# The last column block of three phases of a two-block transformer layer, run one half of the tokens after the other

## The reference, cut to what matters

```python
# first_block, after attention and the gated recurrence (projections gate_a, gate_b)
merged = (sigmoid(gate_a) * (y_attn @ w_attn_branch) + sigmoid(gate_b) * (y_hgrn @ w_hgrn_branch))
x = x + rms_norm(merged @ w_out, g_mix_post)
h = rms_norm(x, g_ffn_pre)
gate, up = split(h @ w_gate_up)
x = x + rms_norm((silu(gate) * up) @ w_down, g_ffn_post)
ple_gate = sigmoid(rms_norm(x, g_ple_pre) @ w_ple_gate)
e = (p @ w_ple_proj) * ple_gate
x = x + rms_norm(e, g_ple_post)

# second_block, twice (l = 0, 1); mod comes from c and w_ada
shift, scale, gate = split(silu(c) @ w_ada[l] + b_ada[l])
h = layernorm(x) * (1 + scale) + shift
u_f, z_f, cq, ckv, k_r, z_a = split(h @ w_in[l])
y = concat([fourier_mix(u_f) * silu(z_f), latent_attention(cq, ckv, k_r) * silu(z_a)]) @ w_out[l]
x = layernorm(ALPHA * x + gate * y) * ln_g[l] + ln_b[l]
```

## Time and profile before

| what | us |
|---|---|
| median of 3 runs | 2385.27 (2381.05 to 2387.98) |
| the profiled execution: device time | 2383.35 |
| its span (first to last instruction) | 2381.5 |
| TensorE busy | 2235.6 (94%) |
| VectorE busy | 1530.5 (64%) |
| ScalarE busy | 1102.9 (46%) |
| GpSimd busy | 103.0 (4%) |

### The profile page before, as it was taken

The page is one execution under the profiler, slowest core; times in us unless marked ns, Lnnn a source line. Parts: engine busy times, 40 slices in busy tenths (PEclk is TensorE's granted clock), DMA queues, the critical chain, the costliest instruction groups (busy, mean ns, idle before and its releaser), DMA issues.

```text
span 2381.5 us, 26442 instructions
## 1 busy us (share of the span) xinstructions
PE 2235.6 (94%) x10514; PEld 1860.3 (78%) x10514; DVE 1530.5 (64%) x1820; ACT 1102.9 (46%) x1497; POOL 103.0 (4%) x97
## 2 busy tenths in 40 slices
PE   8999999999897999999999999796999995999996
PEld 6788888887786788878887888675888774888875
DVE  5665476748776776677777777676365556545555
ACT  5566455433344444444433444555465343545542
POOL 1000000001100000000000001011000002000001
PEclk9999999999999999999999999898999997999998
DMA  6544654477885888888888887673464463544463
GB/s 220 182 133 133 194 168 145 135 242 263 271 275 204 287 279 283 280 288 294 287 283 281 299 282 262 201 248 117 136 189 123 156 232 97 161 151 141 149 230 106
DMA packets 233659, 500.60 MB, mean 210 GB/s; under 512 B 15696, under 2 KB 25600, under 8 KB 232128
## 3 DMA queue, kind: packets, MB, share of 16 engines
q1 hardware_dynamic: 229520, 485.64, 62.4%
q0 software_dynamic: 2416, 11.85, 1.4%
q10 hardware_dynamic: 1600, 1.43, 0.2%
HBM read 496.74 MB, written 2.12 MB: 209 GB/s over the span
## 4 chain that ended last, share of the span: by engine, by line
PE 52%; DMA 18%; issue 11%; DVE 11%; ACT 6%; POOL 1%; SPq 0%; POOLq 0%; ACTq 0%; DVEq 0%
PE bank L210 50%; DMA raw<-in_w_gate_up 7%; DVE wl L231 5%; DMA raw<-in_w_down 4%; ACT wh L227 4%; DVE arena L239 3%; DMA raw<-in_w_out 3%; PE bank L218 2%; DVE arena L231 2%; ACT arena L227 1%; DMA raw<-in_w_ple_gate 1%; DMA raw<-in_w_hgrn_branch 1%; POOL arena L231 1%; DMA raw<-in_w_attn_branch 1%; DMA raw<-in_w_ada 1%
## 5 line engine op out<-in xcount | busy, mean ns | idle before, releaser
L231 DVE TENSOR_TENSOR wl<-raw,wh 128x1024 fp32r<-128x1024 f32 (+1 forms) x732 | 892.2, 1226 | 613.3 <-ACT wh L227 606.5
L227 ACT ACTIVATE wh<-raw 128x1024 fp32r<-128x1024 f32 (+1 forms) x732 | 763.0, 1048 | 957.9 <-PE bank L210 365.3
L210 PE MATMUL bank<-wh,hh 128*128 128x512 f32 (+1 forms) x1616 | 640.9, 397 | 24.4 <-DVE wl L231 8.2
L210 PE MATMUL bank<-wh,hl 128*128 128x512 f32 (+1 forms) x1616 | 629.9, 390 | 0.0
L210 PE MATMUL bank<-wl,hh 128*128 128x512 f32 (+1 forms) x1616 | 629.4, 389 | 0.0
L210 PE MATMUL bank<-wh,ah 128*128 128x512 f32 (+1 forms) x1312 | 515.0, 393 | 17.5 <-DVE wl L231 16.2
L210 PE MATMUL bank<-wl,ah 128*128 128x512 f32 (+1 forms) x1312 | 509.9, 389 | 0.0
L210 PE MATMUL bank<-wh,al 128*128 128x512 f32 (+1 forms) x1312 | 509.8, 389 | 0.0
L210 PEld LDWEIGHTS bank<-wh,hh 128*128 128x128 f32 x1616 | 307.0, 190 | 90.2 <-DVE wl L231 11.6
L210 PEld LDWEIGHTS bank<-wh,hl 128*128 128x128 f32 x1616 | 306.5, 190 | 63.2
L210 PEld LDWEIGHTS bank<-wl,hh 128*128 128x128 f32 x1616 | 307.1, 190 | 59.1
(11 more groups left out here) (100 smaller groups left out, 685.9 us busy)
## 6 DMA issues: line engine op xcount, KB each, us to landing
raw<-in_w_in SPq DMA_DIRECT2D x264, 512.0 KB, 3.8
raw<-in_w_ada SPq DMA_DIRECT2D x192, 512.0 KB, 4.8
raw<-in_w_gate_up SPq DMA_DIRECT2D x176, 512.0 KB, 4.9
raw<-in_w_out SPq DMA_DIRECT2D x96, 512.0 KB, 4.9
raw<-in_w_down SPq DMA_DIRECT2D x88, 512.0 KB, 5.1
raw<-in_w_ple_gate SPq DMA_DIRECT2D x32, 512.0 KB, 5.4
raw<-in_w_attn_branch SPq DMA_DIRECT2D x16, 512.0 KB, 5.0
raw<-in_w_hgrn_branch SPq DMA_DIRECT2D x16, 512.0 KB, 5.2
```

Source lines behind the costliest of these rows:

```text
L210: return put("pe", lambda e: e.matmul(o, l, r, start=start, stop=stop_, skip_group_check=skip), w, sig, size(r) / 2400.0 * (4 if r.dtype = ...
L227: return e.activation(o, i, f, scale=scale, **k)
L231: return put(eng, lambda e: e.tensor_tensor(o, a, b, op), w, cost=vcost(eng, o))
```

## The change

Three blocks now run *by halves*: the last `wo` block (`split="half"`: units 0 to 3 for both halves of the tokens, then units 4 to 7 for m = 0 and again for m = 1), the last `pgate` block and the last `wo2` block of each layer (`split="last"`: all 8 units for m = 0, then all 8 for m = 1). What follows such a block is emitted per half (`ev_post_half`, `ev_pg_last`, `ev_o_last`). So that 8 units of weights can stay, blocks 1 to 3 of these phases borrow the idle operand H as four more slots (`lend`, `release`); the slots are one queue now, and `take_item` is called by their number. The following phase still normalises and starts for all tokens at once (`pre`, whose operand waits for both halves).

The moments of the layer norms come from sums that the additions leave behind (`stt_sum`, with `accum_out`) and from squares on ScalarE (`sq_sum`), in place of `bn_stats`. All wide work of GpSimd goes to VectorE. The `gate` and `pgate` blocks no longer wait for `r` to be emitted, and the squares for it are yielded one by one. The last `down` blocks are added from `quick` (`out_down`). `mixes` are emitted right behind the split block (`mix_now`), and their inputs are loaded by GpSimd's queue during pgate.

```diff
+        def prefetch(l, rel, tk):
...
+            return mixes
...
+        slots = deque((WH[:, i, :], WL[:, i, :], None, None) for i in range(NSPL))
+        unit_slot = []
+
+        def lend(op, end):
+
+            for i in range(4):
+                op.lent[i] = True
+                ks = slice(4 * i, 4 * i + 4)
+                slots.append((op.hi[:, ks, :].rearrange("p k t -> p (k t)"), op.lo[:, ks, :].rearrange("p k t -> p (k t)"),
+                              [op.read[k] for k in range(4 * i, 4 * i + 4)], (op, i, end)))
+
+        def release(g, t):
+            wh, wl, _, lent = unit_slot[g]
+            if lent is None or g < lent[2] - 4:
+                slots.append((wh, wl, [t], lent))
+            else:
+                op, i, _ = lent
+                op.lent[i] = False
+                for k in range(4 * i, 4 * i + 4):
...
+                sl = slots.popleft()
+                wh, wl = sl[0][:, 0:kk * nw], sl[1][:, 0:kk * nw]
+                th = act(wh, raw, ACTF.Copy, t, sl[2])
+                tl = tt(wl, raw, wh.bitcast(F32), ALU.subtract, th, sl[2])
+                unit_slot.append(sl)
...
+            nu = (nk + 1) // 2
+            g0 = gu[0]
+            if borrow is not None:
+                lend(*borrow(g0))
+            if split is None:
+                order = [(u, (0, 1)) for u in range(nu)]
+            else:
+                c = nu - 4 if split == "half" else 0
+                order = [(u, (0, 1)) for u in range(c)] + [(u, (m,)) for m in range(2) for u in range(c, nu)]
+            part = []
+
+            def done(tok):
+                part.append(tok)
+                if len(part) == (2 if split else 1):
+                    acc_free[a] = list(part)
...
+                while ptr[0] < len(stream) and slots and (n < 1 + (at % 3 == 0) or len(unit_slot) <= g + 2):
+                    n += stream[ptr[0]][0] == "g"
...
+                if 1 in ms:
+                    release(g, t)
+                    for q in range(kk):
+                        operand.read[kts[2 * u + q]] = t
...
+                if split and at == nu - 1:
+                    sides.append(evac(acc, t, done, 0, *args))
...
+            if split:
+                sides.append(evac(acc, t, done, 1, *args))
...
-                t = tt(o, GB[n][:, m, :], o, ALU.add, t, hg_tok["ma", n], eng="pool")
+                t = tt(o, GB[n][:, m, :], o, ALU.add, t, hg_tok["ma", n])
...
-                if scale is None:
-                    t1 = act(YR[:, 1, cs], YR[:, 1, cs], ACTF.Copy, t_r, tks, scale=r[:, 1:2])
-                    t1 = tt(XR[:, 1, cs], YR[:, 1, cs], XR[:, 1, cs], ALU.add, t1, x_tok, eng="pool")
-                    t = stt(XR[:, 0, cs], YR[:, 0, cs], r[:, 0:1], XR[:, 0, cs], ALU.mult, ALU.add,
-                            t_r, tks, x_tok)
-                    nxt[n] = [t, t1]
-                    bn_stats(0, n, XR, t)
-                    if n:
-                        bn_stats(1, n - 1, XR, nxt[n - 1])
-                    if n == 3:
-                        nxt["bn"] = bn_stats(1, n, XR, t1)
...
+            nxt["row"] = row_load(row, 0, GR, "row", nxt["y_rd"])
             for m in range(2):
                 for n in range(4):
                     t = square_sum(XR[:, m, n * 512:(n + 1) * 512], SS[:, m, n:n + 1], nxt[n], t_r)
+                    yield
...
+        def ev_post_half(acc, tok, done, m, t_row):
+            while 2 not in y_tok:
+                yield
+            cs = slice(3 * 512, 4 * 512)
+            t1 = square_sum(acc[m][:, :], SS[:, m, 3:4], tok)
+            t = tt(YR[:, m, cs], acc[m][:, :], GR[:, cs], ALU.mult, tok, t1, t_row)
+            done(t)
+            y_tok["h", m] = [t, t1]
+            if m:
+                y_tok[3] = y_tok["h", 0] + y_tok["h", 1]
...
-        until(lambda: "r" in nx)
+        block("wo", H, ALL, ev_post_half, t_row, split="half")
+        chain.append(residual(Y, cols_of("g_ffn_pre"), t_x2, nx, "g_ffn_post"))
...
+            while "r" not in nx:
+                yield
...
+        def out_down(acc, tok, done, n, part):
+            cs = slice(n * 512, (n + 1) * 512)
+            while n not in ya:
+                yield
+            for m in range(2):
+                t = tt(YR[:, m, cs], acc[m][:, :], YR[:, m, cs], ALU.add, tok, ya[n])
+            done(t)
+            y_tok["s", n] = t
...
-                    t1 = tt(YR[:, m, cs], YR[:, m, cs], GR[:, cs], ALU.mult, t, t_row,
-                            eng="dve" if n == 3 else "pool")
+                    t1 = tt(YR[:, m, cs], YR[:, m, cs], GR[:, cs], ALU.mult, t, nx["row"])
...
+            if n == 0:
+                mixg[0] = prefetch(0, now(), mixd[0])
...
+        def ln_half(m, LR, *t):
+
+            ME, V = MV[:, m, :], VE[:, m:m + 1]
+            t = red(ME, SUMS[:, m, :, :], ALU.add, *t)
+            t = ts(ME, ME, 1.0 / D, None, ALU.mult, None, t)
+            t = tt(V, ME[:, 0:1], ME[:, 0:1], ALU.mult, t)
+            t = stt(V, ME[:, 1:2], EPS, V, ALU.add, ALU.subtract, t)
+            return tt(LR, V, CST[:, K_MH:K_MH + 1], ALU.pow, t, eng="pool")
+
+        def stt_sum(o, a, sc, b, op0, op1, acc_, *w):
+            return put("dve", lambda e: e.scalar_tensor_tensor(out=o, in0=a, scalar=sc, in1=b, op0=op0, op1=op1,
+                                                               accum_out=acc_), w, cost=vcost("dve", o))
...
+        def pre(l, x_tok):
+            while len(half_tok[l]) < 2:
+                yield
+            x_tok.extend(now())
+            t = red(MV, SUMS, ALU.add, half_tok[l])
+            t = ts(MV, MV, 1.0 / D, None, ALU.mult, None, t)
+            t = tt(VE, MV[:, :, 0], MV[:, :, 0], ALU.mult, t)
+            t = stt(VE, MV[:, :, 1], EPS, VE, ALU.add, ALU.subtract, t)
+            t = tt(LR, VE, CST[:, K_MH:K_MH + 2], ALU.pow, t, eng="pool")
+            t = stt(NM, MV[:, :, 0], -1.0, LR, ALU.mult, ALU.mult, t)
...
+                         ts(TX[n % 2][:, 1, :], XR[:, 1, cs], LR[:, 1:2], NM[:, 1:2], ALU.mult, ALU.add,
+                            t, rd[n % 2])]
...
+        def ev_pg_last(acc, tok, done, m):
+            while 2 not in y_tok:
+                yield
+            prel, t_rp, t_row = nf["y_rd"], nf["r"], nf["row"]
+            G = G_[1]
+            cs = slice(3 * 512, 4 * 512)
+            t = act(G[:, m, :], acc[m][:, :], ACTF.Sigmoid, tok, t_rp, prel, scale=R1[:, m:m + 1])
+            done(t)
+            t = tt(YR[:, m, cs], G[:, m, :], E_[:, m, cs], ALU.mult, t, e_tok[3], prel)
+            t1 = sq_sum(G[:, m, :], YR[:, m, cs], SS[:, m, 3:4], t)
+            t = tt(YR[:, m, cs], YR[:, m, cs], GR[:, cs], ALU.mult, t1, t_row)
+            yield
+            tks = [z for n in range(3) for z in y_tok[n]] + [t, t1]
+            r, t_r = rstd_of(SS[:, m:m + 1, :], D, tks)
+            for n in range(4):
+                c2 = slice(n * 512, (n + 1) * 512)
+                t = stt_sum(XR[:, m, c2], YR[:, m, c2], r, XR[:, m, c2], ALU.mult, ALU.add, SUMS[:, m, 0, n:n + 1],
+                            t_r, tks)
+                t2 = sq_sum(G[:, m, :], XR[:, m, c2], SUMS[:, m, 1, n:n + 1], t)
+                yield
+            half_tok[0].append([t, t2])
...
+            block("pgate", Y, ALL, ev_pg, n, borrow=last_of(H, 24) if n == 1 else None)
+        until(lambda: (0, 5) in mod_tok)
+        clear(H)
+        block("pgate", Y, ALL, ev_pg_last, split="last")
+        mix_now(0)
...
-                    t = put("dve", lambda e, m=m, n=n, cs=cs: e.bn_stats(BNS[:, m, n, :], Z[:, m, cs]), [t])
-                y_tk[n] = t
+                    t1 = stt_sum(Z[:, m, cs], XR[:, m, cs], ALPHA, Z[:, m, cs], ALU.mult, ALU.add,
+                                 SUMS[:, m, 0, n:n + 1], t)
+                    t2 = sq_sum(JUNK, Z[:, m, cs], SUMS[:, m, 1, n:n + 1], t1, tk["za_done"], late["jk"])
+                    late["jk"] = t2
+                y_tk[n] = [t1, t2]
...
-                    e = "pool" if m and n < 3 - l else "dve"
-                    t = tt(Z[:, m, cs], Z[:, m, cs], LG[:, cs], ALU.mult, tn[n, m], late["g"], eng=e)
-                    tn[n, m] = tt(XR[:, m, cs], Z[:, m, cs], LB[:, cs], ALU.add, t, late["b"],
-                                  eng="pool" if m and n == 3 and l == 0 else e)
...
+            def ev_o_last(acc, tok, done, m):
+                cs = slice(3 * 512, 4 * 512)
+                while 2 not in y_tk:
+                    yield
+                t = tt(Z[:, m, cs], acc[m][:, :], GW[:, cs], ALU.mult, tok, tk["gw"], tk["za_done"])
+                done(t)
+                t = stt_sum(Z[:, m, cs], XR[:, m, cs], ALPHA, Z[:, m, cs], ALU.mult, ALU.add, SUMS[:, m, 0, 3:4], t)
+                t2 = sq_sum(JUNK, Z[:, m, cs], SUMS[:, m, 1, 3:4], t, late["jk"])
+                late["jk"] = t2
+                LR = ST[:, 202 + m:203 + m]
+                t = ln_half(m, LR, t, t2, [y_tk[n] for n in range(3)])
+                yield
+                for n in range(4):
+                    c2 = slice(n * 512, (n + 1) * 512)
```

(20 more changed lines are left out.)

301 lines of the change are left out of this document (158 added, 143 removed).

## The result

The changed kernel takes 2372.04 us (median of 9 runs, 2365.11 to 2378.56), against 2385.69 us for the kernel before on the same chips: a ratio of 0.994, with a 95% interval of 0.9927 to 0.9954. That is 14 us faster where 41 were forecast (39.0 from the profiled execution), and just above the stated range, which ended at 2370.

The account below looks back on a forecast made before the run. The prediction took TensorE as the bound, with about 146 us idle to win. Its terms, 1.5 + 5.8 + 10 + 0 + 6.2 + 6.8 + 8.7 = 39.0, from 2383.35 gave 2344 us; range 2328 to 2370.

Parts of the forecast that it names:

- What bounds the kernel: Whole kernel: TensorE, busy 2235.6 of 2381.5 us, is the bound; only its idle time, about 146 us, can be won.
- GpSimd's wide work moved: Branch and wo stage: 35 operations move to VectorE, hidden away from the ends, and splits get shorter; gain 1.5 us (0 to 4).
- wo to gate: Gap behind wo: shorter chain, earlier first gate unit, and most of three waits for wl gone; gain 5.8 us (2 to 9).
- down to pgate: From down through pproj to pgate: bank free in time, full clock, one transpose group less; gain 10 us (4 to 11).
- pgate: The pgate blocks: borrowed slots let supply run eight units ahead, about 3 us ahead of need; booked 0 (-6 to +4).
- the third rival: Slower: each split also waits for its slot, so the raw buffers' round bounds supply; 2400 us at 0.7 per split; chance 0.05.
- pgate to u: Layer 0, gap behind pgate 20.0 instead of 22.8 us, and mixes out of the first u block; gain 6.2 (0 to 9).
- wo2 to u: Layer 0 to 1, gap behind wo2 22.4 instead of 29.2 us through the halves; gain 6.8 us (0 to 9).
- the tail: Last matmul to the end: only half 1 remains, 14.0 instead of 22.7 us; gain 8.7 us (5 to 10).
- The second rival: The halves don't hide: half 0's additions come late behind splits, pass m=0 may starve; about 2363 us; chance 0.15.
- The doubled addition: First rival: VectorE's addition with a sum takes twice its time, 1.4 us; 2357 us in all; chance 0.13.
- GpSimd: Sign in the profile after: GpSimd busy about 20 us.

Follow-up runs that it names:

- e12: e11 with the last wo block run whole instead of by halves; 2346.17 us, ratio 0.9825 to the kernel before.
- e15: e12 with pgate slots borrowed from the third block on, not everything emitted at once, and pgate's transposes held until four pproj blocks are emitted; 2349.24 us.
- e3: Changed kernel with the addition of the two branches (8 operations of 128x512) back on GpSimd; 2365.22 us, ratio 0.9908 to the kernel before.
- e5: Changed kernel with the last down block's additions emitted ahead of the splits of the third and fourth pproj unit; 2367.35 us, ratio 0.9919.
- e14: e12 with pgate slots borrowed from the third block on, not everything emitted at once, and down's additions back behind the pproj splits; 2343.56 us.
- e2: Changed kernel with the extra slots of the pgate blocks borrowed from the third block on instead of the second; 2361.61 us, ratio 0.9902.
- e11: Changed kernel, branch additions on GpSimd, down's additions earlier, pgate's follow-up emitted at once, one unit supplied in pass m=1 of last pgate and wo2 blocks; 2345.5 us.

## Why the prediction was wrong

- **What bounds the kernel.** Right: TensorE's busy time stayed (2235.6 to 2236.2 us), and all of the difference lies in its idle time, about 146 us before and 129 after.
- **GpSimd's wide work moved**, forecast -1.5, measured +7.3, of which 5 to 6 repeat. This is the first step that failed: that the work leaving GpSimd is "hidden" on VectorE and that shorter splits give time back. The splits did get shorter (mean 1.223 instead of 1.241 us). But the sum priced the operations and took the queues they left and entered as given. With the additions on VectorE, ScalarE's `hh`, and so the `hl` that TensorE waits for at 650 us, stands behind one more copy of weights, which waits for its load (3 us), and an empty GpSimd queue lets the row's load slip forward (1 to 3 us). Nothing in this term looked at the DMA that had stood behind the moved work. The split of the last `wo` block, booked under the next term, costs some 3 us of the stretch too. With the additions back on GpSimd and the block unsplit (`e12` to `e15`) the stretch takes 241.7 to 244.4 us, 1 to 3 less than the 245.0 of the one profile before; whether the 1.5 us of the forecast are in that is open. The Trainium skill ("SBUF — State Buffer", Who interferes with whom) says that a VectorE instruction with two SBUF inputs contends with a GpSimd instruction that reads SBUF; the row agrees (a split of 2.31 instead of 1.24 us), but `e3` and its three followers show that this stretch is some 5 us shorter with the contention than without it.
- **wo to gate**: forecast a gap of 12 to 13 us, measured 12.9; the three waits for `wl` behind it are gone but one of 1.5 us. The size was right and one reason not: without the split the gap is 12.3 and less, so the square and product saved by it were no part. What remains is the earlier first unit and the squares one by one; they were not taken apart. That the size came out is in part luck.
- **down to pgate**, forecast -10, measured -4.1. The prediction reads the wait of 5.93 us as that of the first `pproj` matmul; it is the second unit's, which changes no number. The step that failed is "so the bank is free in time": the wait is still 5.7 us. `out_down` changes who emits the additions, but not that three `pproj` splits stand ahead of them. `e5`, `e14` and `e15` show that taking this wait away doesn't bring the 5.9 and 3.0 us either: the wait for the first transposed columns grows in its place, and the stretch stays at 24 to 26 us. The term asked only where the stall goes, and not what is late next. The group of transposes moved behind the first unit was booked at 1.8, and the gap between the last `pproj` matmul and the first of `pgate` did shrink from 9.1 to 6.3 us.
- **pgate**, forecast 0 (-6 to +4), measured +9.4. The supply was judged by its rate alone, and there it was right (93.3 us in `e2`). What failed is that the term left out what is queued behind the supplied copies: the sigmoids that free the banks, 13.7 us late. This is the mirror of the third rival, which looked for the damage in the rate of the ring and not in what waits behind it. Its sum has a slip: 556 pieces in the 1090 us from 530 to 1620 are one in 1.96 us, not 1.88 to 1.9, so the supply had more room than it says. Together with the first term this one makes 18 of the 23 us that are missing in this profile (39.0 forecast, 16.1 measured), and 16 to 17 of what repeats.
- **pgate to u**, forecast -6.2, measured -6.1, but differently: the gap was 17.7 and not 20.0, and `u` gained 1.1 and not 3.4. The working has the first columns 30.9 us after pass m=0 and they came at 28.6: the steps were together 1.3 us shorter, and the eight sums booked at 1.0 cost almost nothing (below). That the two errors cancel in the total is luck.
- **The rest of layer 0**, forecast nothing, measured -6.7. The `mixes` for layer 1 also moved into a gap. Before, they took 3.70 us inside a `wo2` block and 1.68 us of waiting for their load, in one row of the timeline of TensorE, which the prediction doesn't use. That is 5.4 of the 6.7 us:

```profile
1929.80 3.70 PE L210 MATMUL bank<-arena 128*128 128x512 f32 x8 [1.68 <-DMA arena<-in_w_fmix]
```

- **wo2 to u** forecast 22.4 us, measured 22.5; **the tail** 14.0, measured 12.6. The order of the steps held, but the exact hit at `wo2` is in part luck: the four splits ended 1.4 us later than in the working, since the first waited 1.7 us for its copy, and the nine sums booked at 1.1 us cost almost nothing. The second rival had the mechanism right (half 0's pairs behind four splits), but it was in the sum already: `e11` shows what it cost, 3.6 and 4.8 us.
- **layer 1**, forecast nothing, measured +4.1: 1.9 in `u` and 2.2 up to the last matmul, where a wait for `wl` at the `wo2` blocks takes 3.6 us instead of 3.0. Its cause wasn't tried.
- **The doubled addition** is not the case. The groups by form, VectorE (mean in ns):

```profile
L1557 DVE SCALAR_TENSOR_TENSOR arena<-arena,st 128x512 f32<-128x512 f32 x24 | 17.6, 750 | 1.9 <-POOL st L231 1.4
L1557 DVE SCALAR_TENSOR_TENSOR arena<-arena 128x512 f32<-128x512 f32 x16 | 10.6, 690 | 0.3
L1557 DVE DVE_READ_ACCUMULATOR arena<-arena,st 128x1 f32 x24 | 2.0, 82 | 0.0
```

The addition itself takes 690 ns where the one without a sum took 692, and the accumulator's read 82 ns. That read lies almost wholly in the end of the addition: three additions with a sum in a row start 0.67 to 0.68 us apart (at 1627.98, 1628.65 and 1629.33 us), and four of the same form without one take 2.74 us (at 1511.75), 0.66 us apart. So the sum costs 0.01 to 0.02 us and not the 0.12 that was booked, some 0.3 us for all 22 on the path instead of 2.7. The Trainium skill's sentence ("Vector Engine (DVE) Microarchitecture Reference", Points that are easy to get wrong) that this instruction with two SBUF sources halves throughput isn't borne out by these rows of 32-bit operands.

- **GpSimd** is busy for 36.7 us and not about 20: without its wide work (63.6 and 6.1 us) it was busy for 33 of its 103.0 us already.

The range was missed by 2 us at its upper end, because each unknown was bounded by the price of an operation. None of its bounds allowed for an order in which a cheap operation that frees a bank waits behind expensive ones that nobody needs yet.

## What to carry to other kernels

When weights are fetched further ahead, look at what stands behind the additional copies in the queue of each in-order engine: two operations of 1.3 us together that free banks cost 13.7 us because fourteen copies of later weights stood before them, and at `wo` a wait grew by 3 us with one such copy more before the operation it was for. When work leaves an engine, ask which DMAs that engine issues behind it, since they will start earlier. And overlapping two halves is worth its full price only where nothing else enters the queue between them: 8.1 us in the tail, 2.3 and 2.6 where four splits came between.

## What the runs showed of the hardware

VectorE's read of its accumulator takes 82 ns, ScalarE's 189 ns in the same kernel, and on VectorE an addition with a sum frees the engine only 0.01 to 0.02 us later than one without. Moving eight additions of 128x512 from GpSimd, where they take over 2 us each beside VectorE, to VectorE, where they take 0.7, made a wait of 3.6 us one of 6.8: in this stretch the slower engine was the better place.
